# GpSimd folds the squares of six channel tiles before TensorE sums a norm

## What is computed

```
def rmsnorm(x, g):
    xf = x.astype(jnp.float32)
    y = xf * lax.rsqrt(jnp.mean(xf * xf, axis=-1, keepdims=True) + RMS_EPS)
    return (y * g.astype(jnp.float32)).astype(x.dtype)
...
        h = rmsnorm(x, norm_mem_g[l])
        mem_n = rmsnorm(mem, norm_memsrc_g[l])
        x = x + memory_cross_attention(h, mem_n, mem_wq[l], mem_wk[l], mem_wv[l], mem_wo[l])
        h = rmsnorm(x, norm_ff_g[l])
        x = x + sqrelu_mlp(h, ff_w1[l], ff_w2[l])
...
        u = modulate(rmsnorm_2(h, norm_ff1[l]), sh1, sc1)
        h = h + FFN_RES * g1[:, None, :] * swiglu(u, w_ff1_gate[l], w_ff1_up[l], w_ff1_down[l])
```

## Time and profile before

| | |
|---|---|
| median of 3 runs | 1555.84 us (1553.88 to 1555.86) |
| the profiled execution | 1559.32 us, span 1557.5 us |
| TensorE busy | 1482.0 us, 95% |
| VectorE busy | 1094.0 us, 70% |
| ScalarE busy | 685.3 us, 44% |
| GpSimd busy | 30.3 us, 2% |
| granted TensorE clock, mean | 0.977 |

### The profile page before, as it was taken

The page is one execution under the profiler, slowest core; times in us unless marked ns, Lnnn a source line. Parts: engine busy times, 40 slices in busy tenths (PEclk is TensorE's granted clock), DMA queues, the critical chain, the costliest instruction groups (busy, mean ns, idle before and its releaser), DMA issues.

```text
span 1557.5 us, 21322 instructions
## 1 busy us (share of the span) xinstructions
PE 1482.0 (95%) x8244; PEld 1273.1 (82%) x8244; DVE 1094.0 (70%) x1636; ACT 685.3 (44%) x884; POOL 30.3 (2%) x20
## 2 busy tenths in 40 slices
PE   7999998999999899889999979999999988999997
PEld 6878887888887677778888868887788866888886
DVE  4799365888668576558886769987746757777653
ACT  2322443555324353535553345553444346455542
POOL 0000000000000000000000000000003400000000
PEclk9999999999998899999999999999999998999999
DMA  8544433455874444334558727757644324445451
GB/s 327 186 163 153 158 122 109 143 205 205 282 255 163 162 162 149 136 108 162 189 189 283 277 94 279 281 184 265 222 164 161 110 83 149 163 162 189 147 171 60
DMA packets 60189, 279.27 MB, mean 179 GB/s; under 512 B 6632, under 2 KB 8105, under 8 KB 35274
## 3 DMA queue, kind: packets, MB, share of 16 engines
q1 hardware_dynamic: 55672, 266.49, 49.1%
q10 hardware_dynamic: 4434, 11.64, 2.0%
HBM read 273.89 MB, written 4.19 MB: 179 GB/s over the span
## 4 chain that ended last, share of the span: by engine, by line
PE 83%; DVE 9%; DMA 3%; ACT 3%; issue 1%; ACTq 0%; DVEq 0%; SPq 0%
PE acc L433 40%; PE acc L435 21%; PE acc L454 10%; DMA ada_w<-in_ada 3%; PE stat L602 3%; PE acc L544 2%; DVE wsplit L1455 2%; PE stat L705 1%; PE score L667 1%; PE acc L548 1%; DVE ada_w L1743 1%; PE score L876 1%; PE turned L687 1%; DVE tsum L1607 0%; DVE prob L1701 0%
## 5 line engine op out<-in xcount | busy, mean ns | idle before, releaser
L433 PE MATMUL acc<-hA,wsplit 128*128 128x512 f32 x1728 | 622.7, 404 | 10.9 <-DVE hA L1595 6.7
L435 PE MATMUL acc<-hA,wsplit 128*128 128x256 f32 x1728 | 487.9, 282 | 0.0
L986 ACT ACTIVATE wsplit<-raw 128x2048 fp32r<-128x2048 f32 (+3 forms) x206 | 366.0, 1777 | 208.6 <-PE acc L435 207.1
L1455 DVE TENSOR_TENSOR wsplit<-raw,wsplit 128x2048 fp32r<-128x2048 f32 (+3 forms) x206 | 436.2, 2120 | 11.7 <-ACT wsplit L986 11.7
L433 PEld LDWEIGHTS acc<-hA,wsplit 128*128 128x128 f32 x1728 | 329.4, 191 | 94.5 <-issue 11.3
L435 PEld LDWEIGHTS acc<-hA,wsplit 128*128 128x128 f32 x1728 | 330.8, 191 | 0.3
L433 PE MATMUL acc<-hid,wsplit 128*128 128x512 f32 x864 | 304.6, 395 | 0.0
L435 PE MATMUL acc<-hid,wsplit 128*128 128x256 f32 x864 | 244.4, 283 | 0.0
L433 PEld LDWEIGHTS acc<-hid,wsplit 128*128 128x128 f32 x864 | 163.2, 189 | 34.4
L996 ACT ACTIVATE lowp<-acc 128x512 f32<-128x512 f32 (+1 forms) x126 | 74.0, 588 | 257.3 <-PE acc L435 228.3
L435 PEld LDWEIGHTS acc<-hid,wsplit 128*128 128x128 f32 x864 | 164.3, 190 | 0.4
(11 more groups left out here) (233 smaller groups left out, 1740.5 us busy)
## 6 DMA issues: line engine op xcount, KB each, us to landing
raw<-in_gu SPq DMA_DIRECT2D x44, 1024.0 KB, 4.9
ada_w<-in_ada SPq DMA_DIRECT2D x144, 256.0 KB, 4.7
raw<-in_up SPq DMA_DIRECT2D x32, 1024.0 KB, 4.9
raw<-in_down SPq DMA_DIRECT2D x32, 1024.0 KB, 5.0
raw<-in_dn SPq DMA_DIRECT2D x32, 704.0 KB, 4.1
raw<-in_pw SPq DMA_DIRECT2D x8, 1024.0 KB, 6.2
raw<-in_memk SPq DMA_DIRECT2D x8, 1024.0 KB, 4.8
raw<-in_memv SPq DMA_DIRECT2D x8, 1024.0 KB, 5.3
```

Source lines behind the costliest of these rows:

```text
L433: nc.tensor.matmul(dst.rearrange("p (s t) -> p s t", s=2), w, h, start=start, stop=False, skip_group_check=True)
L435: return nc.tensor.matmul(dst[:, 0:T], lo_w, h[:, 0, :], start=False, stop=stop, skip_group_check=True)
L986: nc.scalar.activation(wsplit[:, slot, 0, 0:elems_of(n)], raw[:, slot, 0:elems_of(n)], ACT.Copy).then_inc(S("w_hi"), 1)
L1455: V.tensor_tensor(wsplit[:, slot, 1, 0:e], src, wsplit[:, slot, 0, 0:e].bitcast(F32), ALU.subtract).then_inc(S("w_lo"), 1)
```

## The change

For ten of the twelve norms (all but `mix0` and `ffa`, listed as `APART`) GpSimd adds up the squares of pairs 0, 1 and 2. ScalarE puts the squares of pair 0 into the first half of `aux`, and those of pairs 1, 2 and 3 into the second, one after the other. GpSimd adds pair 1 to the first half (fold 1, 128x512), then pair 2 (fold 2, 128x512), then the first half's second tile to its first (fold 3, 128x256). TensorE waits for fold 3 and runs one matmul on the folded tile, then two on pair 3. The squares of pairs 2 and 3 wait for folds 1 and 2, and no longer for sums.

```
@@ norm_sums (TensorE)
                 for p in pairs:
+                    if name not in APART and p < 2:
+                        continue
+                    if p == (0 if name in APART else 2) and q > 0:
+
+                        stat_read(q)
+                    if name not in APART and p == 2:
+                        pe.wait_ge(S("norm_folded"), fold_base(name) + FOLDS)
+                        nc.tensor.matmul(stat[:, 0, :], ones[:], aux[:, 0, 0, :], start=True, stop=False)
+                        continue
                     pe.wait_ge(S("norm_sq"), PAIRS * q + p + 1)
-                    if p == 0 and q > 0:
-
-                        stat_read(q)
+                    half = p % 2
                     for j in range(2):
-                        mm = nc.tensor.matmul(stat[:, 0, :], ones[:], aux[:, p % 2, j, :],
+                        mm = nc.tensor.matmul(stat[:, 0, :], ones[:], aux[:, half, j, :],
                                               start=p == 0 and j == 0, stop=p == PAIRS - 1 and j == 1)
                     mm.then_inc(S("norm_stat"), 1)
@@ norm_squares (ScalarE)
-                    if p >= 2:
-
-                        wait("norm_stat", PAIRS * q + p - 1)
-                    nc.scalar.activation(aux[:, p % 2, :, :], src[:, 2 * p:2 * p + 2, :],
+                    half = p % 2 if name in APART else min(p, 1)
+                    if p >= 2 and name in APART:
+
+                        wait("norm_stat", sums_base(name) + p - 1)
+                    elif p >= 2:
+
+                        wait("norm_folded", fold_base(name) + p - 1)
+                    nc.scalar.activation(aux[:, half, :, :], src[:, 2 * p:2 * p + 2, :],
                                          ACT.Square).then_inc(S("norm_sq"), 1)
@@ GpSimd
+            def fold_squares(name):
+
+                fb, sb = fold_base(name), PAIRS * norm_index(name)
+                first = aux[:, 0, :, :]
+                for p in (1, 2):
+                    wait("norm_sq", sb + p + 1)
+                    if p == 2:
+                        wait("norm_folded", fb + 1)
+                    G.tensor_tensor(first, first, aux[:, 1, :, :], ALU.add).then_inc(S("norm_folded"), 1)
+                wait("norm_folded", fb + 2)
+                G.tensor_tensor(aux[:, 0, 0, :], aux[:, 0, 0, :], aux[:, 0, 1, :], ALU.add).then_inc(S("norm_folded"), 1)
```

More of the change, by code:

```diff
@@ L144 @@
 LN_TABLE = 3
+APART = ["mix0", "ffa"]
+FOLDS = 3
 ATTENTIONS = [("mem0", MEM_HEADS, MEM_HEADS), ("fox", HEADS, HEADS // 2), ("mem1", MEM_HEADS, MEM_HEADS),
@@ L173, in norm_index, with sums_base, fold_base @@
     return [n for n, _ in NORMS].index(name)
+def sums_base(name):
+    return sum(PAIRS if n in APART else 1 for n, _ in NORMS[:norm_index(name)])
+def fold_base(name):
+    return FOLDS * sum(n not in APART for n, _ in NORMS[:norm_index(name)])
 def norm_base(name):
@@ L1053, in norm_root @@
                 q = norm_index(name)
-                wait("norm_stat", PAIRS * (q + 1))
+                wait("norm_stat", sums_base(name) + (PAIRS if name in APART else 1))
                 wait("log_table", q + (1 if q < LN_TABLE - 1 else 2))
@@ L2021, in wait @@
                 pool.wait_ge(S(sem), value)
-            for i in range(NL + 1):
-                wait("gla_exp", i + 1)
-                if i:
-                    wait("gla_scores", i)
-                G.tensor_tensor(qe[:], inT[:, 0:2, :], decay[:], ALU.mult).then_inc(S("gla_qk"), 1)
-                G.tensor_tensor(ke[:], inT[:, 2:4, :], decay[:], ALU.mult).then_inc(S("gla_qk"), 1)
+            def fold_squares(name):
[8 more added lines that the diff above has]
+                G.tensor_tensor(aux[:, 0, 0, :], aux[:, 0, 0, :], aux[:, 0, 1, :], ALU.add).then_inc(S("norm_folded"), 1)
+            for name, _ in NORMS:
+                if name in APART:
+                    continue
+                if name == "ffb":
+                    for i in range(NL + 1):
+                        wait("gla_exp", i + 1)
+                        if i:
+                            wait("gla_scores", i)
+                        G.tensor_tensor(qe[:], inT[:, 0:2, :], decay[:], ALU.mult).then_inc(S("gla_qk"), 1)
+                        G.tensor_tensor(ke[:], inT[:, 2:4, :], decay[:], ALU.mult).then_inc(S("gla_qk"), 1)
+                fold_squares(name)
 def bucket_of(dist):
```

1 line of the change is left out of this document (removed).

## The result

The changed kernel takes **1569.97 us** (median of 4 runs, 1563.22 to 1573.36), the kernel before 1555.85 beside it (4 runs, 1553.88 to 1556.5). The ratio is 1.0084, with a 95% interval of 1.006 to 1.0108: slower by 14 us, where the prediction said 7 and ended its range at 1567.0.

A forecast was written before the change was run, and what follows sets the result against it. TensorE, busy 95% of the span, was taken to bound the kernel except where VectorE's order or the `ada_w` loop decides; norm terms summed to -6.8 us, median 1555.8 to 1562.6, range 1554.0 to 1567.0 (8 in 10).

The forecast's parts named there:

- Who goes first: When GpSimd's fold and VectorE's L1524 both want the port, GpSimd was taken; VectorE loses 1.1 to 1.2 us a fold.
- rival 1: VectorE goes first when both want the port: no change, 1555.0 us; chance 0.24.
- `mem`, +2.1: Norm `mem`: folds covered by VectorE's waits in `pw1`, all five matmuls come off the path; gain 2.1 us.
- `memq0`, `ff0`, `ff1`, together -2.8: Deferred norms: folds 1 and 2 stop VectorE before L1524, so TensorE waits before part (1,0); loss 2.8 us together.
- `mixn`, -4.3: Norm `mixn` in `dn1`: TensorE waits for fold 3, 2.3 us lost, plus 2.0 for the fallen clock; largest term.
- `final2`, -0.4: Norm `final2` in `dn2`: 2.1 us saved, against a wait for folds 2 and 3 taken as 2.5; loss 0.4 us.
- `memq1`, -1.6: Norm `memq1`: two folds before L1524 cost 2.3 us, 0.4 to 0.7 comes back from one sum fewer; loss 1.6.
- `fox` +0.5, `final1` -1.2: `down0`: 1.7 us saved, 1 to 1.6 waited, gain 0.5; `down1`: `ada_w` loop decides, stopped L1743s delay loads, loss 1.2.
- `ffb`, +0.9: Norm `ffb`: TensorE saves 0.86 us ahead of the end of `out`, the rest hidden before pair 3's squares; gain 0.9.
- From profile to median: The profiled execution (1559.3 us) was 3.5 above the median, so the forecast 1566.1 became a median of 1562.6 us.
- Fold 3: GpSimd's half-width addition, expected between nothing and 1.29 us, taken as 0.65.
- Rival 4: Folds cost their gross 2.5 us and stop VectorE for as long; seven norms lose about 1 us more: 1570; chance 0.06.

The follow-up runs named there:

- again: The changed kernel once more, without an edit, for a second profile: 1568.77 us, ratio 1.0083.
- saving_alone: The changed kernel without GpSimd's folds, TensorE still at three matmuls a norm (most squares of pairs 0 to 2 left out): 1547.35 us, ratio 0.996.
- mixn_two_behind: The kernel before, nothing folded; in `dn1` the sums of pairs 0, 1 and 2 come two chunks behind in place of one: 1552.39 us, ratio 0.9978.
- covered_three: The changed kernel with only `mem`, `ffb` and `final2` folded, the other nine norms summed as before: 1554.02 us, ratio 0.9988.
- warm_fill: The changed kernel plus small unread matmuls in TensorE's long waits (16 per deferred norm, 40 in `dn1`, 16 in `dn2`): 1564.37 us, ratio 1.0051.
- beside: The kernel before plus GpSimd additions of the folds' shapes on constants, unread, in seven norms; TensorE keeps all sums: 1557.51 us, ratio 1.0017.

## Why the prediction was wrong

The sign and the mechanism were right, the size was half. The forecast -6.8 us stands against -14.1 by the medians and -13.7 in `again` (-13.1 and -12.9 by the ratios).

- **Bound and upper limit.** 50 matmuls of 0.43 us: TensorE's busy time fell by 18.5 us. As an upper limit 21.5 was right; `saving_alone` puts the worth of all at 8 us.
- **Who goes first.** GpSimd, as taken; rival 1 is out. A stop of VectorE costs 1.1 us (1.79 against 0.69), as taken.
- **`mem`, +2.1.** Measured 2.16.
- **`memq0`, `ff0`, `ff1`, together -2.8.** This is the step that failed: measured -7.2 (53.10, 71.62, 71.55 against 51.03, 69.02, 69.02). The wait before part (1,0) was forecast at 3.2 us and is 2.95. What was wrong was "TensorE stands from 289.4 until 292.6, runs the part (1.4), the folded tile (0.43) and pair 3 (0.86), and ends at 295.3": those lengths are of the full clock. TensorE ran them at half clock and the root came at 297.64. With the clock held by fillers, the three norms lose 0.5, 1.2 and 1.0, in sum 2.7, which is the forecast. So 4.4 us of the miss are the clock here. The prediction had weighed a fall of the clock behind a wait in `dn1` alone, though 3 us of wait were forecast in these norms. The trace before showed shorter waits with a fall behind them: the row of `memq1` has 0.77 us for a record that takes 0.47 at full clock, behind waits of 2.12 and 1.84 us, and the clock is 0.50 from 644 to 648.
- **`final2`, -0.4.** The wait was taken as 2.5 and is 2.9; fold 3 alone took 1.99 us there. With the clock holding it is +1.4, with the clock falling -2.6 (195.86 and 199.78 against 197.22).
- **`mixn`, -4.3.** Measured -4.8 and -4.6, and -4.5 folded alone, all against 206.80, the longest of the unchanged segments; that the size fits so well is in part luck. The forecast wait of 7 us is 7.43. That the old wait of 3.57 us "cost nothing in the end" was wrong: `mixn_two_behind` takes the wait and the fall of the clock away, and its segment is 1.9 to 4.9 us shorter.
- **`memq1`, -1.6.** Not settled: the changed kernel's profiles show +1.8 and -0.4, and the segment scatters by more without any fold.
- **`fox` +0.5, `final1` -1.2.** `fox` lost 0.3. `final1` came to 179.60 and 180.34; of the nine profiles with this norm left alone six have 180.62 to 180.74, so against these it gained 0.3 to 1.1; the other three have 181.13, 182.26 and 182.54 (the kernel before). Both signs were wrong, by less than 2.3 us.
- **`ffb`, +0.9.** Its segment, which holds the mixing stage too, is 0.9 and 1.1 us shorter in the two profiles, within what it scatters (230.2 to 232.9 without a fold in `out`).
- **From profile to median.** The prediction took 3.5 us off since the profiled execution before was that far above its median. 1.9 of these were in `final1` (182.54, where 180.63 is usual; one other of nine profiles has it too). The term for `final1` was reasoned from that stretch.
- **Fold 3** was taken as 0.65 and took 1.05 in `ff0`, 0.81 undisturbed; it ends no wait in the deferred norms.

With 180.63 for `final1`, the segments of the one profile of `again` add up to -12.4 us against those of the kernel before (`mem` 2.2, `memq0`, `ff0` and `ff1` -7.3, `memq1` -0.4, `fox` -0.3, `final1` 0.3, `mixn` -4.6, `ffb` 1.1, `final2` -2.6, the start and `ffa` -0.8). The medians differ by 13.7. Rival 4 named the measured time (1570) with the wrong cause: folds cost their gross time on GpSimd, but VectorE is stopped for 1.1 us and not for 2.5.

What stays open is why the clock is down behind a wait in one execution and up in another. The waits are alike to 0.01 us in `dn2` and in `memq1`, and what TensorE did ahead of them is the same program. The six runs of `again` lie between 1559.8 and 1577.28 us, and how much of that scatter is the clock is not shown.

## What to carry to other kernels

Work taken from the busiest engine moves its waits forward: price each wait that it then runs into, and with it the work right behind at the clock that such a wait has left elsewhere in the trace, not only the wait. Work given to GpSimd takes its place between two VectorE instructions that read SBUF twice, and what it stops there may be on the path (here 1.1 us each time), so let it wait for the last of these and run beside one that reads PSUM. And where a sum or another small step stands between chunks, try it a chunk later before rebuilding it: here that one line gave 2.2 us by the medians (1.2 to 5.8 by the interval of the ratio).

## What was not expected of the hardware

- TensorE's clock behind a wait of given length is not fixed. Behind 2.88 and 2.89 us of waiting in `dn2` two records of a sum took 1.19 and 0.67 us. At the two waits of `memq1`, where `covered_three` and `mixn_two_behind` leave it alone, it fell behind 2.13 and 2.08 us (0.50 from 640 to 644) and held behind 2.13 and 2.42 (1.00 throughout).
- Fillers (`warm_fill`) did not always help: with 1.20 us of wait left behind them in `ff0` the clock held, with 4.18 us left in `dn1` it fell.
- A 128x256 addition on GpSimd took 0.72 to 0.81 us when undisturbed, against 1.26 to 1.30 for 128x512: half the columns cost over half.
- An addition of constants (`beside`) stopped VectorE's low part for 0.85 us and one on `aux` for 1.1.
